# Second layer's prompt attention: TensorE's order within a step becomes older values, transposes, new scores

## What is computed

```
for gi, (w, r) in enumerate(((128, 1), (512, 4), (2048, 16))):   # 3 groups, 8 heads of 64 each
    # tokens t, t+r, t+2r, ... form a sequence; in it, blocks of 128 queries
    s = q . k / 8 - slope * r * (i - j)      # against its own and the previous block of 128 keys
    p = exp(s - rowwise max)                 # masked outside the window
    o = p @ v                                # with its row sum kept, groups merged later
```

## Time and profile before

| | us |
|---|---|
| Median of 3 runs | 2598.12 (2597.06 to 2598.16) |
| Profiled execution, its own time | 2599.12 |
| Span of its profile | 2597.3 |
| This stage, from the first S to the last V | 1458.5 to 1622.5 of the span |

### The profile page before, as it was taken

How to read it: one execution, slowest core, us unless ns; L and a number is a source line. 1 busy time by engine, 2 the same in 40 slices (tenths; PEclk the granted TensorE clock), 3 DMA queues, 4 the chain that set the end, 5 groups by cost and what they waited for, 6 DMA issues and landing times. The chain is left out here.

```text
span 2597.3 us, 42354 instructions
## 1 busy us (share of the span) xinstructions
PE 2500.8 (96%) x16451; PEld 2423.1 (93%) x16451; DVE 1004.1 (39%) x1989; ACT 663.3 (26%) x1265; POOL 433.3 (17%) x456
## 2 busy tenths in 40 slices
PE   7999899999999999999999999789999999999997
PEld 7888699999999999999999899469999999999997
DVE  6466535232332232236212466437332232233335
ACT  4345424211110111123100367224220111111113
POOL 2343101101100101101111433421101100100100
PEclk9999999999999999999999999899999999999999
DMA  4010214113111313111211233843111211311312
GB/s 171 20 52 28 76 49 135 40 43 111 48 33 50 112 33 120 41 36 50 87 67 32 94 91 127 300 153 115 46 39 58 97 42 47 106 38 50 113 34 84
DMA packets 67236, 199.26 MB, mean 77 GB/s; under 512 B 7704, under 2 KB 14232, under 8 KB 66360
## 3 DMA queue, kind: packets, MB, share of 16 engines
q1 hardware_dynamic: 66232, 193.17, 22.5%
q0 software_dynamic: 912, 4.85, 0.5%
HBM read 182.21 MB, written 51.05 MB: 90 GB/s over the span
## 5 line engine op out<-in xcount | busy, mean ns | idle before, releaser
L936 DVE TENSOR_TENSOR WL<-RAW,WH 128x1024 fp32r<-128x1024 f32 (+3 forms) x198 | 220.0, 1112 | 1165.4 <-ACT WH L616 1164.8
L1467 PE MATMUL PS<-XH,WH 128*128 128x384 f32 x2832 | 622.9, 330 | 11.7 <-DVE XL L963 8.4
L1467 PE MATMUL PS<-XH,WL 128*128 128x384 f32 (+1 forms) x2736 | 604.7, 329 | 0.0
L1467 PE MATMUL PS<-XL,WH 128*128 128x384 f32 x2640 | 583.0, 329 | 0.0
L466 POOL TENSOR_TENSOR RAW<-RAW,GAIN 128x1024 f32<-128x1024 f32 x114 | 222.2, 1950 | 1656.2 <-DMA RAW<-in_w_gu 1393.2
L1467 PEld LDWEIGHTS PS<-XH,WH 128*128 128x128 f32 x2832 | 486.0, 189 | 13.2 <-issue 12.2
L616 ACT CAST WH<-RAW 128x1024 fp32r<-128x1024 f32 (+3 forms) x198 | 186.8, 945 | 1184.9 <-PE PS L1467 1151.7
L1467 PEld LDWEIGHTS PS<-XH,WL 128*128 128x128 f32 x2736 | 468.7, 188 | 0.0
L1467 PEld LDWEIGHTS PS<-XL,WH 128*128 128x128 f32 x2640 | 451.9, 188 | 0.0
L1467 PE MATMUL PS<-HL,WH 128*128 128x384 f32 (+1 forms) x1041 | 228.6, 327 | 0.0
L1467 PE MATMUL PS<-HH,WL 128*128 128x384 f32 (+1 forms) x1041 | 228.5, 327 | 0.0
(11 more groups left out here) (215 smaller groups left out, 2562.1 us busy)
## 6 DMA issues: line engine op xcount, KB each, us to landing
RAW<-in_w_gu SPq DMA_DIRECT2D x88, 512.0 KB, 3.5
out_bkS<-in_bk_in SPq DMA_DIRECT2D x8, 2032.0 KB
out_bvS<-in_bv_in SPq DMA_DIRECT2D x8, 2032.0 KB
RAW<-in_w_dn SPq DMA_DIRECT2D x32, 384.0 KB, 3.0
KC<-in_bk_in SPq DMA_DIRECT2D x8, 1536.0 KB, 9.4
VC<-in_bv_in SPq DMA_DIRECT2D x8, 1536.0 KB, 7.2
RAW<-in_w_dn SPq DMA_DIRECT2D x32, 320.0 KB, 2.8
XT<-in_xT SPq DMA_DIRECT2D x16, 544.0 KB, 4.8
```

What stands on the lines that cost most here:

```text
L936: nc.vector.tensor_tensor(lo[:, j, 0:nk * P], RAW[:, j, 0:nk * P], hi[:, j, 0:nk * P].bitcast(F32), ALU.subtract).then_inc(S["wl"], 1)
L1467: ins = mm(PS[:, 3 * j + c, 0:width], w[:, j, k * P:(k + 1) * P], x(k, a, width), start=(k == 0 and n == 0), stop=(k == nk - 1 and n == 2))
```

## The change

Within each step of TensorE's program, S(n) moves from the first place to the last, and V and T change places. A step n was S(n), T(n-3), V(n-5); it becomes V(n-5), T(n-3), S(n). The lags, the waits of each operation, the buffers and the other engines' programs stay as they are.

```diff
                 def body(i, prev, cur=True, first=False, prev_first=False):
                     for st in range(8):
-                        if cur:
-                            scores(i, st, widths(st, first), first)
-                        for lag, what in ((LAG, transposes), (PV_LAG, pv)):
+                        for lag, what in ((PV_LAG, pv), (LAG, transposes)):
                             v = (st - lag) % 8
                             own = st >= lag
                             if own and not cur or not own and prev is None:
@@
                             else:
                                 transposes(b, v, widths(v, f))
+                        if cur:
+                            scores(i, st, widths(st, first), first)
                         if finish:
                             finish(i, prev, st, cur)
```

## The result

The changed kernel takes 2638.4 us, median of 6 runs (2637.25 to 2640.86); the kernel before, 2598.14 us in the same comparison. The ratio is 1.0157 with an interval of 1.0147 to 1.0168: **1.6% slower, by 40 us**. The forecast was 2632.9, with a range of 2619 to 2650.

What follows compares the result with a forecast made beforehand. TensorE's own instruction stream was taken as the bound, with a new loop through ScalarE after the change. Groups +10.0, +12.8, +13.2, ramps -0.2, behind the stage -1.0: +34.8 on 2598.1 gives 2632.9 us, range 2619 to 2650.

Steps and rivals of the forecast that it cites:

- Some 39 times: In the stage, V waits for ScalarE's copy, odd units only: 0.7 us each in group 0, 1.1 in group 2.
- The sizes: Loop through ScalarE per pair of steps: 5.13 us for w = 256 (+0.74), 3.36 us for w = 128 (+1.13).
- Release: Loop term from the end of ScalarE's copy to TensorE's next weight load: 0.12 us, could be 0.06 or 0.2.
- VectorE joins the loop: Rival, 8%: statistics copies make VectorE's minimum late by 0.5 us in two even steps per body: +12, 2645 us.
- The fillings: Pipeline filling: T(0) has two S blocks ahead instead of three; +0.3 us in groups 1 and 2.
- Even units hidden, VectorE not in the loop: VectorE's copy of even units is done 2.8 us after S(n+3), before V needs it; room about 1 us.
- T stays covered: T(n) has two steps and a V behind S(n), 5.2 us against some 3.1 needed, so its wait stays hidden.
- The order's own effect: On TensorE, the new sequence of block kinds changes a step by between 0 and -0.05 us.
- Behind the stage: After the stage, SyncE's KC load, waiting for an output copy, goes out some 1 us earlier: -1 us.
- Hidden after all: Rival, 7%: V finds its copy done, TensorE keeps its steps and earns up to 4.8 us: 2593 to 2598.
- The clock: Rival, 10%: TensorE's clock falls to 1.2 GHz in the w = 128 pairs, 14 us in group 2: 2647 us.
- The end of the stage: The stage of score, transpose and V matmuls ends near 1658 instead of 1622.5 in the new profile.

Runs made afterwards that it cites:

- Exchanging two operations on ScalarE: Changed kernel with ScalarE's copy of unit n-3 put ahead of its exponential of unit n: 2604.5 us, ratio 1.0021.
- a delay on ScalarE: Changed kernel with two extra small ScalarE copies ahead of the exponential, at even units: 2659.6 us, ratio 1.0236; at odd units: 2640.4 us, ratio 1.0157.
- four banks: Kernel with only S moved (T, V, S), its transposes using four PSUM banks in turn instead of two: 2627.9 us, ratio 1.0109.

## Why the prediction was right

- **The mechanism.** The loop S, minimum, exponential, copy, V, T, S was named with its members and its place, and V waits for the copy of every odd unit from 1 to 27 of each group. Exchanging two operations on ScalarE removes it (33 us), and a delay on ScalarE counts at even units alone. Shown.
- **"Some 39 times".** It is 42: the 39 pairs and, in each drain, V(27).
- **The sizes.** For w = 256 I had 5.13 us a pair, measured 5.25 (mean from unit 12 to 30); for w = 128, 3.36 against 3.52. These are the terms that were too small, by 0.12 and 0.16 us, and they account for 4 of the 5.5 us that the stage exceeds the forecast. Release (0.05 to 0.18) and V to T (0.83 and 0.39) were right. What was short for w = 256 is the piece from S to the minimum. I took it from units 22 and 78, where the minimum starts 0.60 and 0.50 us behind the last S matmul. In the changed kernel it starts 0.50 to 0.70 us behind in group 2 (units 78 and 72) and 0.60 to 0.87 in group 0, longest in the even steps that follow a statistics copy; in this small measure the rival "VectorE joins the loop" did occur. One row had stood for all. For w = 128 this piece is 0.10 of the 0.16 us, and most of the rest is behind T: the first matmul of S starts 0.34 us behind T's weight load, in the mean, where the sum had 0.22 + 0.06.
- **The fillings.** +1.8 us instead of +0.6, and 1.35 of it in group 0: S(3) came 4.55 us behind S(0) instead of 2.93 (last matmuls), since T(0), now ahead of it, waited 0.97 us for the first exponential. The forecast had taken that as covered. The stay at the lower clock there was also longer, 8.6 us instead of 5.7. The kernel with V and T alone exchanged had that too, without the wait, and its S(4) came 0.25 us later; so most of the 1.35 is the wait.
- **Even units hidden, VectorE not in the loop.** Right in the changed kernel: TensorE never waits for line 1048. But the room was that of the longer loop. With ScalarE's loop opened, VectorE's came out at once, 2.66 us a pair.
- **T stays covered.** Right in effect, for an incomplete reason. The prediction looked at T's wait for its exponential alone, but T(n+2) also hangs on the copy of n through its bank. In the changed order V(n) stands before it and takes the wait, so the sum was not touched. The experiment with S moved alone was mis-forecast for this; four banks took back 10.1 us of its stage.
- **The order's own effect.** Bounded by 0 and -0.05 us a step; it is -0.05, seen where TensorE sets the pace (4.293 against 4.391 us a pair). The reason given, that V to T is 0.06 shorter than V to S, comes from blocks that had just waited or were draining. In a full step without waits and with w = 256 it is the other way round, 0.94 us against 0.89, and the gain is that T's weight load is followed by S's at 0.44 us where V's came at 0.54.
- **Behind the stage.** -0.7 us measured, -1 forecast. The idle time of VectorE ahead of the MG load went from 6.43 to 5.61 us, which fits; but the granted clock of that part also went from 0.87 to 0.89, so the cause isn't shown:

```profile
1671.60 0.17 DVE L1327 TENSOR_TENSOR SM<-MG 128x8 f32<-128x8 f32 x1 [5.61 <-DMA MG<-u]
```

- **The rivals.** Hidden after all: refuted by the waits. VectorE joins: V waits for no copy of VectorE, and the minima behind a statistics copy were late by 0.1 to 0.3 us in group 0, less than the 0.5 of the rival. The clock: stayed at 1.00 with TensorE busy for about 0.7 of a pair in group 2, and fell once the pair was 0.4 us longer. The Trainium skill ("TensorE: Matmul & The Clock Gate", section "A second HAM failure mode: psum-queue depth-cycling") tells of a kernel in which frequent short idle times between matmul groups made the clock swing between its levels. The trace of the changed kernel doesn't agree, with 42 such waits at a granted clock of 1.00; that of the kernel with the delay at even units does, with two falls in group 2.
- **The end of the stage.** It ended at 1659.4 and 1658 was forecast. This is closer than the sum was, by luck: in this profile the stage began 4.3 us earlier.

## What to carry to other kernels

Moving a block in a software pipeline changes no work but changes the distance between a producer and its consumer on every in-order engine. Write down the closed loop through each engine's queue with what stands ahead of the needed operation there, and divide its length by the number of steps it spans; here the largest quotient, not the busiest engine, gave the step. Where odd and even steps differ, see that the loop comes back to a step of its own kind. Count a buffer that is reused (here a PSUM bank) as a member of the loop as well. And where a copy frees the next step, try it ahead of the work that can wait: here it was worth 33 us in the changed kernel and 3 in the stage of the kernel before.

## What the runs showed of the hardware

- The granted clock held its upper level through 195 us in which TensorE waited 0.5 to 1.2 us in every second step. In the kernel with waits of up to 1.6 us (busy 15.5 of 24 us) it dropped to 0.50 for 6.8 us, twice.
- Where TensorE itself sets the pace, a step in the order S, V, T takes 2.147 us and in the order S, T, V 2.196 (w = 256); for w = 128 it is 1.067 against 1.112. The same blocks, 0.05 us a step apart: 5 us in 96 steps if nothing else binds.
